# Expert rows of three token tiles read two expert steps early and patched by gathers of the missing rows, with another order of the final sums, in a fused decoder layer

## What is computed

```python
top_v, top_i = lax.top_k(e_logits, EXPERT_TOPK)
top_w = jax.nn.softmax(top_v, axis=-1) * p_g
...
for e in range(N_EXPERTS):
    hid = jax.nn.silu(jnp.dot(h, w_gate[e])) * jnp.dot(h, w_up[e])
    y = y + gates[:, e:e + 1] * jnp.dot(hid, w_down[e])
...
x = x + gate_m[:, None] * y
return rms_norm(x, g_final)
```

## Time and profile before

| | us |
|---|---|
| median of 3 runs | 1015.87 (1013.1 to 1015.96) |
| profiled execution, its own time | 1011.23 |
| span of the profiled execution | 1009.4 |
| busy: PE / DVE / ACT / POOL | 953.4 / 594.8 / 400.8 / 119.0 |
| mean granted TensorE clock | 0.987 |
| DMA | 189.88 MB, mean 188 GB/s |

### The profile page before, as it was taken

How to read it: one execution, slowest core, us unless ns; L and a number is a source line. 1 busy time by engine, 2 the same in 40 slices (tenths; PEclk the granted TensorE clock), 3 DMA queues, 4 the chain that set the end, 5 groups by cost and what they waited for, 6 DMA issues and landing times.

```text
span 1009.4 us, 15052 instructions
## 1 busy us (share of the span) xinstructions
PE 953.4 (94%) x5352; PEld 520.2 (52%) x5352; DVE 594.8 (59%) x1597; ACT 400.8 (40%) x909; POOL 119.0 (12%) x218
## 2 busy tenths in 40 slices
PE   3899999999999999999999999999899999989984
PEld 2464575444448756677766455557433434323421
DVE  3489647999999798987777234365322223312227
ACT  6130236666650488777668121212211112211113
POOL 2001000000008411110000000000111111111004
PEclk9999999999999999999999999997999999999998
DMA  9997101111111000050000410199699999999889
GB/s 325 333 358 274 43 22 32 32 42 25 39 43 27 1 1 2 1 190 2 1 2 1 167 63 22 46 412 385 252 406 421 421 417 421 420 421 419 339 334 365
DMA packets 70381, 189.88 MB, mean 188 GB/s; under 512 B 10200, under 2 KB 37136, under 8 KB 58016
## 3 DMA queue, kind: packets, MB, share of 16 engines
q1 hardware_dynamic: 62320, 171.06, 44.4%
q0 software_dynamic: 5760, 16.78, 4.2%
q10 hardware_dynamic: 2224, 1.05, 0.4%
HBM read 174.17 MB, written 18.89 MB: 191 GB/s over the span
## 4 chain that ended last, share of the span: by engine, by line
PE 65%; DVE 20%; DMA 6%; issue 4%; SPq 2%; ACT 1%; POOL 1%; POOLq 0%; DVEq 0%; ACTq 0%
PE PS L2024 12%; PE PS L1901 11%; DVE BIAS L1161 8%; PE PS L2047 6%; PE PS L1794 6%; PE PS L1837 5%; PE PS L1859 4%; DMA X<-in_w_down_dram 3%; PE PS L1755 3%; PE PS L1707 3%; PE PS L1854 2%; DVE X L1225 2%; PE PS L1732 2%; PE PS L2011 2%; PE PS L1672 1%
## 5 line engine op out<-in xcount | busy, mean ns | idle before, releaser
L1707 PE MATMUL PS<-HT,X 128*128 128x512 f32 x384 | 168.8, 593 | 0.0
L2024 PE MATMUL PS<-QKV,HT 128*32 128x512 f32 (+2 forms) x560 | 116.0, 607 | 6.3 <-DMA X<-in_w_up_dram 3.9
L1707 PEld LDWEIGHTS PS<-HT,X 128*128 128x128 f32 x384 | 72.5, 190 | 92.4 <-issue 92.2
L873 ACT ACTIVATE X<-X,nmx 128x128 f32<-128x128 f32 (+7 forms) x128 | 98.4, 770 | 51.6 <-DVE nmx L1225 51.0
L1901 PE MATMUL PS<-QKV,HT 128*128 128x512 f32 x256 | 113.7, 597 | 0.0
L1161 DVE TENSOR_SCALAR_CACHE_REDUCE BIAS<-SC,W 128x384 f32<-128x384 f32 (+3 forms) x128 | 96.4, 810 | 1.1
L1519 DVE TENSOR_TENSOR HT<-PS,HT 128x256 f32<-128x256 f32 x20 | 8.5, 425 | 147.8 <-ACT HT L977 147.8
L856 ACT ACTIVATE X<-SC,W 128x896 f32<-128x896 f32 x64 | 69.6, 1088 | 43.1 <-DVE W L1149 43.1
L1794 PE MATMUL PS<-QKV 64*128 64x512 f32 (+3 forms) x384 | 79.0, 517 | 1.6 <-DVE nmx L1225 1.1
L1901 PEld LDWEIGHTS PS<-QKV,HT 128*128 128x128 f32 x256 | 47.4, 190 | 53.7 <-issue 53.6
L1837 PE MATMUL PS<-ident,X 128*128 128x128 f32 x432 | 63.2, 279 | 2.2 <-DVE X L1243 2.1
(11 more groups left out here) (306 smaller groups left out, 1533.7 us busy)
## 6 DMA issues: line engine op xcount, KB each, us to landing
QKV<-in_w_down_dram SPq DMA_DIRECT2D x20, 1024.0 KB
QKV<-in_w_gate_dram SPq DMA_DIRECT2D x19, 1024.0 KB
QKV<-in_w_up_dram SPq DMA_DIRECT2D x19, 1024.0 KB
QKV<-in_w_ada_dram SPq DMA_DIRECT2D x8, 2048.0 KB, 14.5
QKV<-in_w_ada_dram SPq DMA_DIRECT2D x8, 1024.0 KB, 12.8
X<-in_w_in_dram SPq DMA_DIRECT2D x16, 512.0 KB, 3.8
X<-in_w_down_dram SPq DMA_DIRECT2D x8, 1024.0 KB, 28.0
QKV<-expert_rows SPq DMA_DIRECT2D x16, 512.0 KB, 10.7
```

Source lines behind the costliest of these rows:

```text
L873: act.activation(sc, sc, ACT.Exp, bias=nmx[:, i % 4, m:m + 1], scale=-1.0, accum_out=rs[:, i, m:m + 1]).then_inc(exp_done, 1)
L1707: end = pe.matmul(PS[:, 2 * b + half, :], WS[:, b, j, :], HT[:, j, BANK * half:BANK * (half + 1)], start=(j == 0), stop=(j == KC - 1))
L2024: end = pe.matmul(PS[at, 2 + b, :], hgT[b][:, P * c_ + at.start:P * c_ + at.stop], WGU[w][:, c_, :, :], start=(c_ == 0), stop=(c_ == KC - 1))
```

## The change

Before step 18 is scattered (`LATE` = 18 of 20), SP waits for the scatters of steps 0 to 17 and reads the expert rows of tiles 0, 1 and 2 (`AHEAD` = 3, six transfers). POOL's scatter of step 18, and so that of 19 behind it, waits until these reads have landed. When all scatters have landed, POOL issues six gathers, one for each of the three tiles and each k, which bring only the rows whose slot is in step 18 or 19; a row number of -1 is out of bounds and skipped. The row numbers come from three small DVE instructions (`late_rows`), and the first 384 rows of both halves of `expert_rows` are filled from `x` beforehand. SP then reads the five other tiles in the order 3, 4, 5, 7, 6. The tiles of `mixed` become 0, 1, 2 and 6; squares, roots, finishes and outputs go in the order 3, 0, 4, 1, 5, 2, 7, 6. Places in SBUF move with it.

```diff
@@ -360,9 +360,10 @@
                              "ht_sb", "dn_ps", "y_sb", "rows_out"))
-        yg_in = [sem(f"yg_in{i}") for i in range(T)]
-        cb_done, fin_sq, fin_done, fin_out, diag_done, mix_ps = (
-            sem(n) for n in ("cb_done", "fin_sq", "fin_done", "fin_out", "diag_done", "mix_ps"))
+        yg_in = [sem(f"yg_in{i}") for i in range(5)]
+        yg_ahead, yg_late = sem("yg_ahead"), [sem(f"yg_late{i}") for i in range(3)]
+        cb_done, fin_sq, fin_done, diag_done, mix_ps = (
+            sem(n) for n in ("cb_done", "fin_sq", "fin_done", "diag_done", "mix_ps"))
@@ -380,9 +381,18 @@
         gfin = BIAS[:, 2, :]
-        mixed = (0, 2, 4, 6)
-        diag = SC[:, 0:1024].rearrange("p (i k n) -> p i k n", i=4, k=2)
-        yg = [[QKV[:, D * (2 * i + k):D * (2 * i + k + 1)] for k in range(2)] for i in range(T)]
+        LATE = NSTEP - 2
+        AHEAD = 3
+        read = (3, 4, 5, 7, 6)
+        last = (3, 0, 4, 1, 5, 2, 7, 6)
+        mixed = (0, 1, 2, 6)
+        diag = HF[:, 0:1024].rearrange("p (i k n) -> p i k n", i=4, k=2)
+        squared = HF[:, 2048:2048 + D]
+        yg_home = [QKV[:, 12288:14336], QKV[:, 14336:16384], SC[:, 0:2048]] + [QKV[:, 2048 * i:2048 * (i + 1)] for i in range(5)]
+        yg = [[a[:, D * k:D * (k + 1)] for k in range(2)] for a in yg_home]
+        slot_early = SC[:, 4 * S + 2 * NT:4 * S + 2 * NT + 2 * EARLY]
+        own_row = SC[:, 4 * S + 2 * NT + 2 * EARLY:4 * S + 2 * NT + 4 * EARLY]
+        late_row = slot_early.bitcast(U32)
@@ -514,6 +524,8 @@
             sp.dma_start(wgr[:, :, NG:NR], w_router[0].rearrange("(j p) n -> p j n", p=P)).then_inc(wgr_in, 16)
+            for k in range(2):
+                sp.dma_start(y_dram[S * k:S * k + P * AHEAD, :], x[0, 0:P * AHEAD, :]).then_inc(yg_ahead, 16)
             sp.wait_ge(qk_done, NA)
@@ -575,6 +587,12 @@
             down_load(sp, expert_of(6), 6)
+            def expert_rows(t, landed):
+
+                for k in range(2):
+                    row = S * k + P * t
+                    sp.dma_start(yg[t][k], y_dram[row:row + P, :]).then_inc(landed, 16)
+
             for n in range(NSTEP + 1):
@@ -587,6 +605,11 @@
                             sp.dma_start(XT[:, t, :], h2_dram[P * t:P * (t + 1), :]).then_inc(x2_back, 16)
+                    if n == LATE:
+                        for b in range(2):
+                            sp.wait_ge(y_out[b], 16 * (LATE // 2))
+                        for t in range(AHEAD):
+                            expert_rows(t, yg_ahead)
             sp.wait_ge(route_done, 2)
@@ -608,14 +631,12 @@
             sp.wait_ge(rows_out, 1)
-            for t in range(T):
-                for k in range(2):
-                    row = S * k + P * t
-                    sp.dma_start(yg[t][k], y_dram[row:row + P, :]).then_inc(yg_in[t], 16)
-            for t in range(T):
-                sp.wait_ge(fin_done, t + 1)
-                sp.dma_start(out[0, P * t:P * (t + 1), :], XT[:, t, :]).then_inc(fin_out, 16)
-            sp.wait_ge(fin_out, 16 * T)
+            for i, t in enumerate(read):
+                expert_rows(t, yg_in[i])
+            for i, t in enumerate(last):
+                sp.wait_ge(fin_done, i + 1)
+                sp.dma_start(out[0, P * t:P * (t + 1), :], XT[:, t, :]).then_inc(x2_back, 16)
+            sp.wait_ge(x2_back, 16 * T + 16 * T)
@@ -741,9 +762,12 @@
             pool.wait_ge(route_done, 2)
+            pool.wait_ge(yg_ahead, 32)
             for n in range(NSTEP):
...
                     gather(n + 4)
+                if n == LATE:
+                    pool.wait_ge(yg_ahead, 32 + 32 * AHEAD)
                 scatter(n)
@@ -757,9 +781,16 @@
             pool.sem_inc(rows_out, 1)
-            for t in range(T):
+            pool.wait_ge(route_done, 3)
+            for t in range(AHEAD):
+                for k in range(2):
+                    pool.indirect_dma_start(out=yg[t][k], out_offset=None, in_=y_dram,
+                                            in_offset=bass.IndirectOffsetOnAxis(
+                                                ap=late_row[:, EARLY * k + t:EARLY * k + t + 1], axis=0),
+                                            bounds_check=2 * S - 1, oob_is_err=False).then_inc(yg_late[t], 16)
+            for i, t in enumerate(last):
                 mean = ss[:, 3 * T + t:3 * T + t + 1]
-                pool.wait_ge(fin_sq, t + 1)
+                pool.wait_ge(fin_sq, i + 1)
                 link(pool.tensor_tensor(mean, mean, eps_row[:, t:t + 1], ALU.add))
@@ -1006,17 +1037,17 @@
                                    ).then_inc(diag_done, 1)
-            for t in range(T):
+            for n, t in enumerate(last):
                 if t in mixed:
...
                 else:
-                    act.wait_ge(cb_done, t // 2 + 1)
+                    act.wait_ge(cb_done, read.index(t) + 1)
                     whole = XT[:, t, :]
-                if t:
-                    act.wait_ge(fin_sq, t)
-                act.activation(HF[:, 0:D], whole, ACT.Square, scale=D ** -0.5,
+                if n:
+                    act.wait_ge(fin_sq, n)
+                act.activation(squared, whole, ACT.Square, scale=D ** -0.5,
                                accum_out=ss[:, 3 * T + t:3 * T + t + 1]).then_inc(fin_sq, 1)
@@ -1387,8 +1418,9 @@
                 link(dve.tensor_tensor(pair, pick[:, :, now, :], at.unsqueeze(1).to_broadcast([P, 2, n, NE]), ALU.mult))
-                link(dve.tensor_reduce(slot_col[:, both].rearrange("p (k t) -> p k t", k=2), pair, AX_X, ALU.add))
-                one_hots(link, q0, n, NSTEP, slot_col[:, both],
+                slots = slot_col[:, both] if q0 else slot_early
+                link(dve.tensor_reduce(slots.rearrange("p (k t) -> p k t", k=2), pair, AX_X, ALU.add))
+                one_hots(link, q0, n, NSTEP, slots,
                          (reached[:, 0:2 * n * (NSTEP + 1)], count_row[:, both], row_row[:, both]),
@@ -1539,9 +1571,20 @@
+            def late_rows():
+
+                link(dve.tensor_scalar(own_row.rearrange("p (k t) -> p k t", k=2),
+                                       first_tok[:, :].rearrange("p (k t) -> p k t", k=2)[:, :, 0:EARLY], tok1[:, 0:1], None,
+                                       ALU.add))
+                link(dve.scalar_tensor_tensor(out=own_row, in0=slot_early, scalar=float(P * LATE), in1=own_row, op0=ALU.is_ge,
+                                              op1=ALU.mult))
+                link(dve.tensor_scalar(late_row.bitcast(I32), own_row, -1.0, None, ALU.add))
+                dve.sem_inc(route_done, 1)
+
             dve.wait_ge(modc_set, 1)
...
             weigh_experts()
+            late_rows()
             dve.wait_ge(out_row_in, 32)
@@ -1568,7 +1611,7 @@
                 y1, y2 = yg[t]
-                dve.wait_ge(yg_in[t], 32)
+                dve.wait_ge(yg_in[read.index(t)], 32)
                 link(dve.scalar_tensor_tensor(out=XT[:, t, :], in0=y1, scalar=w1[:, t:t + 1], in1=XT[:, t, :],
@@ -1580,22 +1623,19 @@
                     whole = PS[:, 2 * i:2 * i + 2, :].rearrange("p a n -> p (a n)")
-                dve.wait_ge(rstd_done, rstd_out + t + 1)
+                dve.wait_ge(rstd_done, rstd_out + last.index(t) + 1)
                 dve.scalar_tensor_tensor(out=XT[:, t, :], in0=whole, scalar=ss[:, 3 * T + t:3 * T + t + 1], in1=gfin,
...
-            combine(1)
+            combine(3)
+            combine(4)
+            finish(3)
+            combine(5)
             finish(0)
-            combine(3)
-            finish(1)
-            finish(2)
-            combine(5)
-            finish(3)
             finish(4)
-            finish(5)
             combine(7)
-            finish(6)
-            finish(7)
+            for t in last[3:]:
+                finish(t)
@@ -2093,7 +2133,7 @@
             for i, t in enumerate(mixed):
-                pe.wait_ge(yg_in[t], 32)
+                pe.wait_ge(yg_late[t] if t < AHEAD else yg_in[read.index(t)], 32)
                 add_into(i, diag[:, i, 0, :], yg[t][0], False, False)
```

## The result

The changed kernel takes 1023.82 us (median of 8 runs, 1020.81 to 1026.57) against 1015.91 us for the kernel before (8 runs, 1013.1 to 1017.43): ratio 1.0082, 95% interval 1.0065 to 1.0098. It is 7.9 us slower. The forecast was 1017.7 us, within 1014.0 to 1022.5: the sign was right, the size was not, and the time lies outside the range.

A forecast was written before the change was run, and what follows sets the result against it. Bound: PE's expert products to 969 us, then the last scatter, expert-row reads and final sums on busy DMA engines. R at 981.4, plus 26.8 and 3.0, ends at 1011.2 (+1.8 us); on the median 1017.7, range 1014.0 to 1022.5.

The forecast's parts named there:

- The new wait: POOL's scatter of step 18, held for the early reads, starts at about 976.9 instead of 966.37; R 7.3 us later.
- R: The moment SP issues its first read behind `rows_out`: 974.11 before, forecast 981.4, ends 979.9 and 983.0.
- X0: The moment SP issues its first read of normalised rows; a start other than 953.9 was to show all wrong.
- Early reads: Six transfers, 3.15 MB, moved ahead of R: 8.0 us of reading less behind it, last landing at about 976.8.
- the first rival: Early reads land before 966.4, so the scatter of step 18 is not held: 5.5 us less; chance 0.10.
- The gathers: Six on POOL from R on, 1.02 us each; 7.5 us from start to landing, ends 3.3 and 9.8.
- DVE's chain: At the end DVE starts with the first pair, 5.0 us behind R, and ends at R + 26.3.
- The clock: PE idle before R: low clock costs the two identity sums 1.7 us, ending before the gathers land: nothing.
- the rival: PE at the lower clock through the products of tiles 0 and 1: +9.2 us in all; chance 0.13.
- The sign named for the rival: Granted clock at 0.50 while tile 1 is summed was to show that the lower-clock rival had come true.
- The last tile: End of PE's chain, last square's start to last finish's end: 3.35 us, giving R + 26.8.
- What costs nothing: Fillings on idle engines behind the router's weights, `late_rows` in DVE's 7.15 us wait for ACT: no cost.

The follow-up runs named there:

- ahead1: The changed kernel reading one tile ahead instead of three (`AHEAD` = 1, order 3, 4, 1, 5, 2, 7, 6): 1018.47 us, ratio 1.0025.
- no_gather: The changed kernel without the six gathers and the three instructions that make their lists: 1020.69 us, ratio 1.0053.
- The experiment: The changed kernel with scatter 18 not held; late rows of tiles 0 to 2 go to a place of their own: 1020.35 us, ratio 1.0039.
- warm: The changed kernel with 22 and 10 unread matmuls added where PE waits: 1021.62 us, ratio 1.0047; again 1021.16, ratio 1.007.

## Why the prediction was wrong in size

The step that failed most is "The new wait": R was put 7.3 us later and came 10.2 later, because the sum let the held scatter follow the last byte of the early reads at once. The start of the gathers, the clock and the last tile were too small as well. Step by step, counted from X0, forecast first.

- **Early reads: right in place, 2 us short in the landing.** Issued 9.8 us from X0, at 966.47, within the 960 to 967 named. The share was 1.0 until 978, so they filled no idle time, and the first rival (5.5 us faster) did not come true; `ahead1` and `no_gather` show the same (1.02 from 972 to 974 and from 974 to 976). The 8.0 us of the prediction are bytes on full engines, and no run here saved them. But the last early read should have landed at X0 + 22.9 and did at X0 + 24.8. The bytes were counted right: the shares of 978 to 981 (0.87, 0.40, 0.11) add up to 1.4 us of full engines, which ends at X0 + 22.7. What was left out is that the share fades out over some microseconds before the last read has landed. In the changed kernel profiled again it is at 0.73, 0.18, 0.13 and 0.03, and the read lands at 984.92:

```profile
981.00:982.00 1.00, 0.00 (x0) 0.00 (x0) 0.00 (x0) 0.00 (x0) 0.00 (x0) 1.00 0.73 291
982.00:983.00 1.00, 0.00 (x0) 0.00 (x0) 0.00 (x0) 0.00 (x0) 0.00 (x0) 1.00 0.18 74
983.00:984.00 1.00, 0.00 (x0) 0.00 (x0) 0.00 (x0) 0.00 (x0) 0.00 (x0) 1.00 0.13 53
984.00:985.00 1.00, 0.00 (x0) 0.00 (x0) 0.00 (x0) 0.00 (x0) 0.00 (x0) 0.72 0.03 12
```

- **The new wait: R 10.2 us later instead of 7.3. This is the step that failed.** Beside the 2 us, POOL started 0.76 us after the landing (981.47 to 982.23), the two scatters stood 1.28 us apart for 1.1, and the second took 3.5 us to its landing for 3.32. R came at X0 + 30.4 for X0 + 27.5: **2.9 us** of the miss, and the largest term. (Of the 10.2 us about 1 is the profile of before: in the three other kernels with all reads behind `rows_out` R stands at 21.13 to 21.49, not at 20.19.) The experiment prices the whole hold at 4.4 us.
- **The gathers: right in length, late in start.** They took 7.5 to 9.0 us from issue to landing, 7.9 in the middle, for the 7.5 taken, although they bring 0.35 MB together (the indirect DMAs of the whole execution move 17.13 MB, and 16.78 in `no_gather`). What was missed is the start: tile 0's second gather started at R + 2.2 and not at R + 1.1, since POOL took 0.85 us from R to the first and 1.34 from one to the next (1.04 busy and 0.30 of issue). Tile 0's products came at R + 10.1 for R + 8.6: **1.5 us**. These are the rows that give it, from the groups by line:

```profile
L787 POOL DMA_INDIRECT QKV<-expert_rows,SC x4: 987/1004/1041, 987.9 to 991.9; - x4
...
DMA to landing us min/median/max: 7.5/7.9/9.0
```

- **DVE's chain: right, in part by luck.** The first combine started at R + 5.0 and the second pair's at R + 8.2, for 5.0 and 8.0. Without the gathers DVE ended at R + 26.9 for R + 26.3, but it began at R + 6.6 there and took 20.3 us for the 21.3 forecast: two misses that nearly cancel.
- **The clock: it does cost, but not in the way of the rival.** PE stood still for 10.8 us before R, and the granted clock was at 0.50 from about 980 to 990. In `warm`, with PE busy before R but for the last 1.35 us, it was at 1.00 from 975 to 1015. The forecast put the cost at nothing because the low clock would be over before the gathers land. It was: full at 990, with tile 0's products at 997.14. But PE then stood still once more, for 4.94 us, and the clock was at 0.50 again from 997 to 1000, three of the five microseconds of tile 0. The sign named for the rival, 0.50 while tile 1 is summed, did not come: the clock was at 1.00 from 1001 on, and in the second profile of the changed kernel too the last slow products are tile 0's (0.50 from 1002 to 1004, 0.54 in the next microsecond, 1.00 after it). The rival had two whole tiles at 0.50, 7.4 us. The four tiles took 15.5 us for 14.8 forecast, where `warm` took 14.0 with the clock at 1.00: **0.7 us** against the forecast, and 1.5 us against `warm`. The two cases were kept apart, each with a chance of its own, where what came lies between them.
- **The last tile.** From its square's start to its finish's end it took 4.06 us (1012.69 to 1016.75) for 3.35, **0.7 us**; the finish waited 0.71 for POOL, whose addition of the epsilon took 0.93 us for 0.19 before the change. Why it did, no run shows.
- **What costs nothing:** fillings, `late_rows`, order of sums. Right, within what a measurement can tell.

1.8 forecast + 2.9 + 1.5 + 0.7 + 0.7 = 7.6 us, for 7.7 in the profiles and 7.9 in the medians. That it meets them within 0.3 us is luck, since it is laid against one profile of before, and such profiles differ by up to 3 us. Every one of the mis-sized terms fell to the same side. They were single steps of one chain (landing, POOL's start, scatter, gather's issue, landing, clock), and each had been taken at its bare duration, without the time between. The upper end taken for R was X0 + 29.1, and R came 1.3 us behind even that; the clock and the last tile were in no end of the range.

What stays open: why the early reads' tail is 2.1 us long in one execution and 2.8 in another of the same kernel, and why the price of the clock is 1.6 us in the profiles and up to 3.6 in the medians.

## What to carry to other kernels

Transfers that were put ahead of other work on full DMA engines (a share of 1.0) saved nothing here: look at the DMA share of the stretch into which they go, not at whether the compute engines have work there. If a write has to be held until such a read has landed, count the wait on the critical path with the tail of the read (2.1 to 2.8 us here), the start of the write behind it (0.76 us), its landing (3.5 us for the second scatter) and the engine that falls idle behind it (10.8 us of PE, in which the clock went to 0.50), since here the chain of transfers cost its landings and not only its bytes. A patch of few rows cost nearly the landing of a full gather (7.9 us for 9.1); the estimate from these two is that it pays only where that landing is covered.
